# Decode rows of four token-major projections: high and low part in one stationary tile

## The reference, cut to what matters

```python
h = modulate(rms_norm(x, lw['norm_attn']), sh1, sc1)
parts = split_in(h @ lw['w_in'])
```

## Time and profile before

| | us |
|---|---|
| median of 3 runs | 2227.39 (2226.86 to 2228.37) |
| the profiled execution, its own time | 2228.51 |
| its span, first to last instruction | 2226.6 |
| PE busy | 2141.9 (96% of the span) |
| DVE busy | 1189.7 (53%) |
| ACT busy | 669.7 (30%) |
| POOL busy | 586.5 (26%) |

### The profile page before, as it was taken

One profiled execution on the slowest core, in us unless ns is written; L12 is line 12 of the kernel. 1 busy time (PEld: TensorE's weight loads), 2 busy tenths in 40 slices (PEclk: granted clock), 3 DMA queues, 4 the chain that ended last, 5 costly groups with the idle time before them and its releaser, 6 DMA issues.

```text
span 2226.6 us, 34346 instructions
## 1 busy us (share of the span) xinstructions
PE 2141.9 (96%) x13481; PEld 1956.2 (88%) x13481; DVE 1189.7 (53%) x2155; ACT 669.7 (30%) x1407; POOL 586.5 (26%) x367
## 2 busy tenths in 40 slices
PE   8999898999989999999999999999999999999999
PEld 3798786676666899999999999899999999999998
DVE  5774275888976167764211333655445444454445
ACT  3332365777763134432002112331110011100112
POOL 0112112545651155541000113422221112211120
PEclk9999898999999999999999999999999999999999
DMA  9021353000035312222232543221111111111112
GB/s 363 18 99 38 93 178 137 1 1 1 1 112 203 119 29 59 59 68 59 76 90 81 176 109 98 67 78 38 57 39 39 57 39 57 38 39 57 38 39 79
DMA packets 175589, 168.62 MB, mean 76 GB/s; under 512 B 10194, under 2 KB 156083, under 8 KB 170116
## 3 DMA queue, kind: packets, MB, share of 16 engines
q1 hardware_dynamic: 167462, 117.96, 17.8%
q0 software_dynamic: 7760, 48.55, 6.6%
q10 hardware_dynamic: 224, 0.08, 0.0%
HBM read 152.98 MB, written 17.87 MB: 77 GB/s over the span
## 4 chain that ended last, share of the span: by engine, by line
PE 63%; DVE 2%; POOL 1%; issue 1%; ACT 0%; POOLq 0%; ACTq 0%
PE psall L244 19%; PE psall L246 18%; PE psall L245 18%; PE psall L2416 2%; PE psall L2051 2%; DVE work L2297 1%; PE psall L2078 1%; POOL work L1973 0%; PE psall L2093 0%; PE psall L2060 0%; PE psall L3152 0%; PE psall L2086 0%; PE psall L2095 0%; DVE work L2602 0%; DVE work_short L2614 0%
## 5 line engine op out<-in xcount | busy, mean ns | idle before, releaser
L244 PE MATMUL psall<-hT_short,ring_short 128*128 128x344 f32 x1896 | 615.0, 324 | 5.6 <-DVE ring_short L239 3.4
L246 PE MATMUL psall<-hT_short,ring_short 128*128 128x344 f32 x1896 | 608.0, 321 | 0.0
L239 POOL TENSOR_TENSOR ring_short<-ring,ring_short 128x1024 fp32r<-128x1024 f32 (+3 forms) x52 | 196.1, 3773 | 1069.0 <-DVE ring_short L234 757.6
L245 PE MATMUL psall<-work_short,ring_short 128*128 128x344 f32 x1392 | 445.4, 320 | 0.0
L244 PEld LDWEIGHTS psall<-hT_short,ring_short 128*128 128x128 f32 x1896 | 359.0, 189 | 6.3 <-issue 6.2
L246 PEld LDWEIGHTS psall<-hT_short,ring_short 128*128 128x128 f32 x1896 | 358.5, 189 | 0.0
L245 PEld LDWEIGHTS psall<-work_short,ring_short 128*128 128x128 f32 x1392 | 262.2, 188 | 0.2
L3313 DVE SCALAR_TENSOR_TENSOR xT<-psall,mod,xT 128x344 f32<-128x344 f32 (+1 forms) x264 | 151.3, 573 | 132.6 <-PE psall L246 129.1
L245 PE MATMUL psall<-xT_short,ring_short 128*128 128x344 f32 x648 | 208.6, 322 | 0.0
L3193 ACT ACTIVATE work<-psall 128x344 f32<-128x344 f32 (+1 forms) x66 | 30.0, 457 | 502.5 <-PE psall L246 501.7
L244 PE MATMUL psall<-work_short,work_short 128*128 128x344 f32 x528 | 177.7, 337 | 3.5 <-POOL work_short L239 2.9
(11 more groups left out here) (460 smaller groups left out, 4015.7 us busy)
## 6 DMA issues: line engine op xcount, KB each, us to landing
ring<-in_w_up SPq DMA_DIRECT2D x44, 512.0 KB, 5.0
ring<-in_w_in SPq DMA_DIRECT2D x27, 512.0 KB, 3.8
work<-in_ada_w SPq DMA_DIRECT2D x23, 512.0 KB, 4.2
work<-in_w_down SPq DMA_DIRECT2D x10, 1024.0 KB, 5.0
ring<-in_ada_w SPq DMA_DIRECT2D x9, 512.0 KB, 4.3
x_spill<-xT SPq DMA_DIRECT2D x4, 1032.0 KB, 14.8
xT<-x_spill SPq DMA_DIRECT2D x4, 1032.0 KB, 7.3
ring<-in_ada_w SPq DMA_DIRECT2D x4, 1024.0 KB, 14.6
```

What stands on the lines that cost most here:

```text
L239: return eng.tensor_tensor(lo, src, hi, ALU.subtract)
L244: pe.matmul(out, w[0], x[0], start=first, stop=False)
L245: pe.matmul(out, w[0], x[1], start=False, stop=False)
L246: return pe.matmul(out, w[1], x[0], start=False, stop=last)
```

## The change

The decode tokens' stationary tile becomes 72 columns wide: the high part in columns 0 to 7, zeros, and the low part in columns 64 to 71. Each slice k then needs two matmuls (this tile by the weights' high part and by their low part) in place of three. Rows 0 to 7 and 64 to 71 of the sum are two parts, which have to be added: ACT copies rows 64 to 71 to SBUF, and DVE adds rows 0 to 7 to it (`join`). For groups 0 to 2 the result, `dec_sum`, is what ACT squares and DVE scales in place of the PSUM rows. For group 3 the sum goes straight to `vhi`, and SP waits for it before it stores `hi_rows`. The product of the two low parts is now in the sum as well.

```diff
 stage_token_major
+    dec_moved, dec_joined = s.sem("t_dec_moved"), s.sem("t_dec_joined")
+    dec_part, dec_sum = view(s.work, 24880, 512)[0:NB], view(s.work, 25392, 512)[0:NB]
...
             sp.wait_ge(copied, UNITS)
+            sp.wait_ge(dec_joined, 4)
             sp.dma_start(T["hi_rows"], s.vhi[0:NB, TT, :]).then_inc(sent_v, 16)
...
 tensor
+                    if t == TT:
+                        for part in (w_hi, w_lo):
+                            last = pe.matmul(s.ps[u % n_psum][0:HD + NB, 0:w], norm.dec[:, k, :], part[g][:, k, :],
+                                             start=(k == 0 and part is w_hi), stop=(k == KT - 1 and part is w_lo))
+                    else:
+                        last = product(...)
...
 scalar
                 act.wait_ge(mm, u + 1)
+                if t == TT:
+                    act.activation(dec_part[:, 0:groups[g][1]] if g < 3 else sq[0][0:NB, :],
+                                   ps[HD:HD + NB, 0:groups[g][1]], ACT.Copy).then_inc(dec_moved, 1)
+                    if g < 3:
+                        act.wait_ge(dec_joined, g + 1)
+                        ps = dec_sum
                 if g == 3:
-                    ch.link(act, act.activation(s.vhi[0:n, t, :], ps[0:n, :], ACT.Copy))
+                    if t < TT:
+                        ch.link(act, act.activation(s.vhi[0:n, t, :], ps[0:n, :], ACT.Copy))
...
 vector
+            def join(g):
+                v.wait_ge(dec_moved, g + 1)
+                w = groups[g][1]
+                part, out = (dec_part, dec_sum) if g < 3 else (sq[0][0:NB, :], s.vhi[0:NB, TT, :])
+                v.tensor_tensor(out[:, 0:w], s.ps[(g * NT + TT) % n_psum][0:NB, 0:w], part[:, 0:w],
+                                ALU.add).then_inc(dec_joined, 1)
...
+                if t == TT:
+                    join(g)
+                    ps = dec_sum
                 v.wait_ge(squared, u + 1)
...
             inputs.index(v)
+            join(3)
...
 FirstNorm
+        self.dec = s.spare_short(0, KT, HD + NB)
...
         ch.link(v, high(v, s.hT[:, :, dec], x))
-        low(v, s.xT_r[:, :, dec], x, s.hT[:, :, dec]).then_inc(self.dec_ready, 1)
+        ch.link(v, v.memset(self.dec.bitcast(F32), 0.0))
+        high(v, self.dec[:, :, 0:NB], x)
+        low(v, s.xT_r[:, :, dec], x, s.hT[:, :, dec])
+        low(v, self.dec[:, :, HD:HD + NB], x, s.hT[:, :, dec]).then_inc(self.dec_ready, 1)
```

More of the change, by code:

```diff
@@ L673, in _ @@
                 for k in range(KT):
-                    last = product(pe, s.ps[u % n_psum][0:n, 0:w], (s.hT[:, k, cols], s.xT_r[:, k, cols]),
-                                   (w_hi[g][:, k, :], w_lo[g][:, k, :]), k == 0, k == KT - 1)
+                    if t == TT:
[3 more added lines that the diff above has]
+                    else:
+                        last = product(pe, s.ps[u % n_psum][0:n, 0:w], (s.hT[:, k, cols], s.xT_r[:, k, cols]),
+                                       (w_hi[g][:, k, :], w_lo[g][:, k, :]), k == 0, k == KT - 1)
                 last.then_inc(mm, 1)
```

## The result

Over 20 runs each, the median is 2233.03 us with the change and 2227.28 us before it. The ratio is 1.0018, with a 95% interval of 1.0012 to 1.0025: the change costs 4.0 us (2.7 to 5.6). That is just under the 0.2% that the prediction set as its bound for a difference; the interval reaches above it. The forecast was 2230.4 us. By the ratio the time is 2227.28 x 1.0018 = 2231.3 us, inside the range. The plain medians differ by more, 5.75 us, and the one with the change lies 0.03 us above the range's upper end of 2233.0 us. All ratios here are of executions in the core's usual state; one of E9 (2360 us) and one of E3 (2970 us), at a much lower granted clock, are left out.

What follows compares the result with a forecast made beforehand. PE was taken as the bound, busy 2141.9 of 2226.6 us, held at its seams by POOL's low parts. 0.0 us without the clock plus 3.0 us for two falls gave 2230.4 us, range 2226.0 to 2233.0.

Steps and rivals of the forecast that it cites:

- Products: PE in units 8, 17, 26 and 35: 8 matmuls fewer each, 6.56 us in all, the 72-column tile free.
- Seam 0 to 1: PE's passage into group 1: start at 110.87, 0.71 us won and 1.14 us turned into a wait.
- DVE's chain at unit 8: Addition, ACT's square and hand-overs ahead of DVE's reduce: 1.37 us longer, bounds 0 and 2.0 us.
- Seam 1 to 2: PE's passage into group 2: 1.10 us later, at 153.58, its wait growing from 0.73 to 3.9 us.
- Unit 17's chain is hidden: In group 2, DVE's added chain of about 1.3 us hides, as DVE waits 1.78 us in unit 23.
- Seam 2 to 3: PE's passage into group 3: 1.10 us later, its wait growing from 1.34 to 2.8 us.
- End of the stage: Unit 35 saves 1.85 us in full; DVE's addition ahead of the `hi_rows` store costs 0.7 us.
- Sum without the clock: Whole stage: +1.10 - 1.85 + 0.7 = 0.0 us, nothing left of 6.56 us.
- The clock: TensorE falls to half clock behind the waits ahead of groups 2 and 3: 1.5 us each, +3.0 us.
- all is won: Rival: the seams do not hold PE up; -5.9 us, 2221.5 us, chance 0.04.
- the chain is hidden: Rival: addition and square cost DVE nothing at unit 8, or its slack is larger; about -1.4 us, chance 0.08.
- The long falls: Rival: a long half-speed stretch behind each of the two waits, 3.1 to 3.3 us each; +6.4 us, chance 0.13.

Runs made afterwards that it cites:

- E9: The unchanged kernel of the change, executed again: ratio 1.0016 against the kernel before, next stage 3.89 us later.
- E3: The change, with PE running 19 and 11 unused products in the waits ahead of groups 2 and 3: ratio 1.0009, next stage 0.04 us earlier than before.
- E1: The kernel before with the new form in unit 35 alone: ratio 1.0003, next stage 1.24 us earlier.
- E2: The kernel before, three products per slice kept, with the copy and join added in all decode units: ratio 1.0001, next stage 3.43 us later.
- E5: The kernel before with the new form in unit 8 alone: single execution, 2232.00 us, next stage 2.72 us later.
- E6: The kernel before with the new form in unit 17 alone: single execution, 2227.92 us, next stage 0.03 us earlier.
- E10: E3 repeated, beside E9 on one chip: ratio 0.9997 against the kernel before, next stage 0.05 us earlier.
- E8: The kernel before, with POOL making and signalling each low part in four pieces: ratio 0.9989, next stage 2.59 us earlier.
- E7: The change, with POOL making and signalling each low part in four pieces: ratio 0.9973 against the kernel before, next stage 5.23 us earlier.
- E4: The change, with DVE rounding the next group's weights three units earlier: ratio 0.9993 against the kernel before, next stage 3.16 us earlier.

## Why the prediction was right

The stage was forecast 3.0 us late and is 4.0; the time +3.0 us, measured +4.0 (2.7 to 5.6). Step by step, positions in the trace of the change:

- *Products*: 16 of 512 columns fill 245.99 to 249.84 with 15 steps of 0.23 us. The 72 columns are free, as taken; E1 shows it alone.
- *Seam 0 to 1*: PE was forecast at 110.87 and starts at 110.88. The wait of 1.1 us shows as 0.81, because the profile counts it from the end of the turned tiles' row.
- *DVE's chain at unit 8*: forecast 1.37 us; 117.61 to 118.98 is 1.37. E2 and E5 show that this chain by itself makes group 2 late.
- *Seam 1 to 2*: forecast 153.58 with a wait of 3.9 us; measured 153.60 and 3.83. The hit is close by some luck: of the slack of 0.27 us, 0.08 was none, because DVE idles 0.23 us ahead of this rounding with the change as well, and POOL's row came out 0.11 us shorter.
- *Unit 17's chain is hidden, its saving lost*: E6, -0.03 us.
- *Seam 2 to 3*: PE sets the pace of group 2; the wait was forecast at 2.8 us and is 2.76.
- *End of the stage*: forecast -1.85 + 0.7 = -1.15; E1 measured -1.24.
- *Sum without the clock*: forecast 0.0; E3 and E10 measured -0.04 and -0.05.
- *The clock*: two falls, as forecast. The term that was mis-sized is "half of some 3.2 us is lost, 1.5 us" for the first one. By the count from POOL's first row, group 3's rounding is 3.73 us late (187.89 - 104.04 against 184.11 - 103.99). The seam makes 1.07 us of it, so the first fall cost 2.66 us; its half-speed stretch lasted 6.8 us, in both profiles of the change. Group 3 then starts 3.69 us late. Its last product ends 3.35 us late although 1.85 us of products were saved on the way, so the second fall cost 1.5 us. Together that is 4.2 us, where 3.0 were counted.

So the falls follow from waits that the chain and the early PE make; the 72-column products are not slow by themselves (E1, E3).

That the clock would fall behind both waits was right in both profiles of the change, but the reason given for the shorter one was weak. It rested on the wait of 2.88 us that ended at 1440.59. The change does not touch that code, and the wait comes again in all twelve traces of this case, at 2.85 to 2.89 us. The clock fell behind it in three of them (the kernel before, E1, E2). In the profile of the change it did not; timeline of PE and window:

```profile
1447.75 0.43 PE L244 MATMUL psall<-work_short,work_short 128*128 128x344 f32 x1 [2.89 <-POOL work_short L239]
```
```profile
1444.60:1452.00 7.40, 4.51 (x29) 4.25 (x28) 7.37 (x8) 3.00 (x5) 4.13 (x3) 1.00 0.01 2
```

The wait of 3.44 us ahead of 1043.52, in contrast, had its fall in all twelve. So the second fall was not as sure as the forecast had it, and that it came in both profiles is in part luck. The rule of thumb of the Trainium skill, "TensorE: Matmul & The Clock Gate", section "HAM oscillation — how this bites in real kernels", would have left out the second fall. The window at 200.60 here, and E5's fall behind 2.54 us, go against it; the row at 1447.75 agrees with it.

The rivals: that all is won and that the chain is hidden are both refuted (E2, E5). The long falls came true for one wait of two. That case was priced at 6.4 us for both, and one of them explains the missing 1.0 us. The argument against it was a misreading: the 21 records at 1440 follow one another without a gap from 1440.59 on, at half speed, just as here. Two sums are slightly off. The range's upper end adds up to 2232.8 us (3.3 + 1.5 + 0.6), not 2233.0, and the 219 records of group 3 include unit 35 and the turned tiles, so 192 of them are the products in question. Between unit 14's reduce and the rounding for group 2 lie ten more rows of that unit, not two.

## What to carry to other kernels

Work taken off the busiest engine is worth something only up to its next hand-over: read in the trace when the operand of the next group became ready, and let the saving stop there. A short step added to an engine that is behind is paid by whoever waits for its next product, here a rounding 27 us later. Where a group must wait for prepared operands, pass them on in pieces. Here that won 2.6 us in the kernel before (E8), and beside it the change, a loss of 4.0 us otherwise, was a gain of 2.6 (E7).

## What was not expected

How long the clock stays at half, and whether it falls at all, depends on more than the wait's length. In this stage it was at half for 6.8 us behind 3.83 and 3.85 us, both times begun inside the wait, and for 3.4 us behind 2.76 us (twice), 2.54 us (E5), 2.44 us (E4) and 1.96 us (E2). Behind 2.03 us (E6) it did not fall, nor behind nine of the twelve waits near 2.88 us later in the program. So waits from about 2 to 2.9 us went either way in these runs. What decides there, and what makes a stretch long, stays open.
